# Scaling of the scan's gated groups on ScalarE, other rates of the scan beside the z and memory blocks, and the third head's values two tiles later

## The reference

```python
# first block: the mixer's state-space branch, 32 heads of 64 in 4 groups
z, xbc, dt_f, dt_b, q, k, v, gates = split_cols(h @ w_in, IN_SPLITS)
...
y = y_fwd + y_bwd + d_skip.reshape(SSD_GROUPS, SSD_HPG, 1).astype(xh.dtype) * xh
y = gated_group_rmsnorm(y.reshape(b, s, SSD_INNER), z, ssd_norm_g)
branch_ssd = y @ w_br_ssd
...
def gated_group_rmsnorm(y, z, g):
    v = (y * jax.nn.silu(z)).astype(jnp.float32).reshape(bsz, s, SSD_GROUPS, d // SSD_GROUPS)
    v = v * lax.rsqrt(jnp.mean(v * v, axis=-1, keepdims=True) + EPS)
    return (v.reshape(bsz, s, d) * g.astype(jnp.float32)).astype(y.dtype)
...
# in both blocks, after the mixer: attention over the memory, 4 heads of 256
q = (h @ w_q).reshape(b, s, XATTN_HEADS, XATTN_HEAD_DIM)
scores = jnp.einsum('bqhd,bkhd->bhqk', q, k).astype(jnp.float32) * (XATTN_HEAD_DIM ** -0.5)
probs = jax.nn.softmax(scores, axis=-1).astype(v.dtype)
out = jnp.einsum('bhqk,bkhd->bqhd', probs, v).reshape(b, s, D_MODEL)
return out @ w_o
```

## Time and profile before

| | |
|---|---|
| runs | 2428.92, 2428.44, 2429.64 us |
| profiled execution | 2428.55 us, its span 2426.7 us |
| TensorE (PE) busy | 2396.6 us, 99% |
| its weight loads (PEld) | 1953.8 us, 81% |
| VectorE (DVE) busy | 1262.5 us, 52% |
| ScalarE (ACT) busy | 1001.5 us, 41% |
| GpSimd (POOL) busy | 328.7 us, 14% |
| mean DMA rate | 104 GB/s |
| chain that ended last | PE 93%, DVE 3%, ACT 1% |

### The profile page before, as it was taken

One profiled execution on the slowest core, in us unless ns is written; L12 is line 12 of the kernel. 1 busy time (PEld: TensorE's weight loads), 2 busy tenths in 40 slices (PEclk: granted clock), 3 DMA queues, 4 the chain that ended last, 5 costly groups with the idle time before them and its releaser, 6 DMA issues.

```text
span 2426.7 us, 30328 instructions
## 1 busy us (share of the span) xinstructions
PE 2396.6 (99%) x12040; PEld 1953.8 (81%) x12040; DVE 1262.5 (52%) x1897; ACT 1001.5 (41%) x1628; POOL 328.7 (14%) x254
## 2 busy tenths in 40 slices
PE   8999999999999999999999999999999999999998
PEld 7777778777888888888888888888887888888887
DVE  5688746478764455444333544333677555433422
ACT  7766654235563344333223333222544444322321
POOL 0000000555100101111102111100022201111100
PEclk9999999999999999999999999999999999999999
DMA  6221325323665232332322332222322232333321
GB/s 202 77 70 46 93 96 179 110 78 110 194 204 206 96 105 70 104 98 89 98 98 96 96 105 91 91 96 87 112 62 69 78 113 80 94 96 104 104 96 53
DMA packets 171486, 251.65 MB, mean 104 GB/s; under 512 B 11344, under 2 KB 88400, under 8 KB 171344
## 3 DMA queue, kind: packets, MB, share of 16 engines
q1 hardware_dynamic: 170192, 247.61, 32.1%
q10 hardware_dynamic: 1152, 2.10, 0.2%
HBM read 231.83 MB, written 16.78 MB: 102 GB/s over the span
## 4 chain that ended last, share of the span: by engine, by line
PE 93%; DVE 3%; ACT 1%; issue 1%; DMA 0%; POOL 0%; SPq 0%; POOLq 0%; DVEq 0%; ACTq 0%
PE bank L1132 92%; PE bank L1236 1%; DVE wlo L1946 1%; PE bank L1259 0%; DVE T L1954 0%; ACT xp L1797 0%; PE bank L1360 0%; ACT whi L1478 0%; DMA zb<-scr_z 0%; DVE macc L1946 0%; DVE W L1946 0%; PE bank L1384 0%; PE bank L1195 0%; DVE ml L1954 0%; DMA raw<-in_w_in 0%
## 5 line engine op out<-in xcount | busy, mean ns | idle before, releaser
L1132 PE MATMUL bank<-xh,whi 128*128 128x512 f32 x1784 | 709.8, 398 | 7.9 <-DVE wlo L1946 7.9
L1132 PE MATMUL bank<-xh,wlo 128*128 128x512 f32 x1784 | 696.2, 390 | 0.0
L1132 PE MATMUL bank<-xl,whi 128*128 128x512 f32 x1784 | 695.4, 390 | 0.0
L1946 DVE TENSOR_TENSOR wlo<-raw,whi 128x1024 fp32r<-128x1024 f32 (+2 forms) x406 | 500.7, 1236 | 338.0 <-ACT whi L1478 337.7
L1478 ACT ACTIVATE whi<-raw 128x1024 fp32r<-128x1024 f32 (+2 forms) x406 | 419.4, 1038 | 516.4 <-PE bank L1132 509.5
L1132 PEld LDWEIGHTS bank<-xh,whi 128*128 128x128 f32 x1784 | 335.4, 188 | 94.4 <-issue 20.2
L1132 PEld LDWEIGHTS bank<-xh,wlo 128*128 128x128 f32 x1784 | 335.1, 188 | 71.3
L1132 PEld LDWEIGHTS bank<-xl,whi 128*128 128x128 f32 x1784 | 335.8, 188 | 65.2
L1946 DVE TENSOR_TENSOR T<-bank,R 128x512 f32<-128x512 f32 x86 | 59.0, 688 | 344.3 <-PE bank L1132 344.3
L1132 PE MATMUL bank<-hh,whi 128*128 128x512 f32 x528 | 205.4, 389 | 0.0
L1132 PE MATMUL bank<-hl,whi 128*128 128x512 f32 x528 | 205.4, 389 | 0.0
(11 more groups left out here) (353 smaller groups left out, 3486.4 us busy)
## 6 DMA issues: line engine op xcount, KB each, us to landing
raw<-in_w_in SPq DMA_DIRECT2D x92, 512.0 KB, 3.6
raw<-in_w_ffn_in SPq DMA_DIRECT2D x88, 256.0 KB, 3.2
raw<-in_ffn_gate SPq DMA_DIRECT2D x88, 256.0 KB, 2.8
raw<-in_ffn_up SPq DMA_DIRECT2D x88, 256.0 KB, 3.1
raw<-in_ffn_down SPq DMA_DIRECT2D x44, 512.0 KB, 3.6
raw<-in_w_ffn_out SPq DMA_DIRECT2D x22, 512.0 KB, 3.5
raw<-in_w_xattn_kv SPq DMA_DIRECT2D x16, 512.0 KB, 4.3
raw<-in_w_kv_mem SPq DMA_DIRECT2D x16, 512.0 KB, 4.8
```

The source lines that it names most:

```text
L1132: return e.matmul(out, l, r, start=start, stop=stop, skip_group_check=skip)
L1946: return e.tensor_tensor(out, a, b, op)
```

## The change

The scaling of a group is split in two: `y_inverse` (VectorE's reciprocal) keeps the old place, and `y_scale` becomes four ScalarE copies with a scale, two points later. The scan's rate is 3.5 instead of 3.6 beside `z0` to `z2`, 2.8 beside `z3`, and 2.0 instead of 1.9 beside the memory's blocks. In the attention over the memory `v2`, `t3` and `v3` come two tiles later.

```diff
             for g in means:
                 step("y_mean", g)
-                soon(2, "y_scale", g)
+                soon(2, "y_inverse", g)
+                soon(4, "y_scale", g)
...
-        scan = start(ssd(), 3.6)
+        scan = start(ssd(), 3.5)
         for g in range(4):
             if g == 3:
+                scan[1] = 2.8
                 start(prepare(1, 4), 4)
             gemm(f"z{g}", ev_z(g))
         pace[0] = 0.5
-        scan[1] = 1.9
+        scan[1] = 2.0
...
-                for what in ("t0", "t1", "v0", "", "v1") if hs[0] == 0 else ("t2", "", "v2", "t3", "", "v3"):
+                for what in ("t0", "t1", "v0", "", "v1") if hs[0] == 0 else ("t2", "", "", "", "v2", "t3", "", "v3"):
...
@@ in scalar() @@
+            def y_scale(g):
+                w.wait_ge(*at("y inverse", g))
+                for c in range(4):
+                    ins = copy(xg[g][:, c, :], xg[g][:, c, :], ss[:, 4 * g + c:4 * g + c + 1])
+                ins.then_inc(*up("y_act", ("y scaled", g)))
...
@@ in vector() @@
-            def y_scale(g):
+            def y_inverse(g):
                 s = ss[:, 4 * g:4 * g + 4]
                 w.wait_ge(*at("y sqrt", g))
                 e.reciprocal(s, s).then_inc(*up("y_scaled", ("y inverse", g)))
-                w.wait_ge(*at("y inverse", g))
-                for c in range(4):
-                    ins = ts(xg[g][:, c, :], xg[g][:, c, :], s[:, c:c + 1], None, ALU.mult)
-                ins.then_inc(*up("y_scaled", ("y scaled", g)))
```

More of the change, by code:

```diff
@@ L1927, in scalar @@
                     "o_split": o_split, "dt": dt, "cum": cum, "difference": difference, "cb": cb, "state": state_, "decay": decay, "z_out": z_out,
-                    "z_square": z_square, "y_mean": y_mean, "y_turn": y_turn, "bs_out": bs_out, "m_split": m_split,
+                    "z_square": z_square, "y_mean": y_mean, "y_scale": y_scale, "y_turn": y_turn, "bs_out": bs_out, "m_split": m_split,
                     "mv_out": mv_out, "kv_split": kv_split, "xq_out": xq_out, "x_scores": x_scores, "x_turn": x_turn, "x_pv": x_pv, "ffn_gate": ffn_gate,
@@ L2647, in vector @@
                     "state": state_, "decay": decay, "decayed": decayed, "y_add": y_add, "across": across_, "z_silu": z_silu, "z_gate": z_gate,
-                    "y_mean": y_mean, "y_scale": y_scale, "y_turn": y_turn, "bs_out": bs_out, "bs_lo": bs_lo, "m_lo": m_lo, "m_sum": m_sum,
+                    "y_mean": y_mean, "y_inverse": y_inverse, "y_turn": y_turn, "bs_out": bs_out, "bs_lo": bs_lo, "m_lo": m_lo, "m_sum": m_sum,
                     "mk_out": mk_out, "kv_lo": kv_lo, "xq_out": xq_out, "x_scores": x_scores, "x_turn": x_turn, "x_scale": x_scale, "x_pv": x_pv,
```

## The result

| | before | after |
|---|---|---|
| median of 8 runs each, side by side | 2428.93 us (2428.44 to 2429.64) | 2436.32 us (2435.44 to 2437.72) |
| ratio | | 1.0031, 95% interval 1.0021 to 1.0040 |
| profiled execution | 2428.55, span 2426.7 | 2435.53, span 2433.7 |
| TensorE's idle time, all waits over 0.05 us added up | 22.95 us | 25.17 us |
| granted clock at 1.2 GHz, the end of the program left out | nowhere | three stretches of 3.41 us, from 597.9, 604.7 and 676.4 |

The kernel is 7.4 us slower, outside the predicted range and on the other side. The span grew by 7.0 us, of which TensorE's idle time is 2.2; the other 4.8 are in its busy time.

The account below looks back on a forecast made before the run. TensorE, busy 2396.6 of 2426.7 us, was taken to bound the kernel; 3.3 + 1.6 + 1.1 - 2.1 + 0.1 = 4.0 us gained gave 2424.9 us. Own range 2423 to 2427; 8 in 10, 2419.0 to 2428.4.

Parts of the forecast that it names:

- Attention, +3.3: Attention over the memory: moving v2, t3 and v3 two tiles later removes both TensorE waits for xpl, gaining 3.3 us.
- Scaling, +1.6: Scaling moved to ScalarE: the 1.64 us wait at spread in mkv10 goes with nothing lost, gaining 1.6 us.
- z2, +1.1: Third z block: with points at 3.5 the wlo comes a point earlier, gaining 1.1 of the 1.28 us wait.
- z3 and mkv10, -2.1: Fourth z block and first mkv10 tiles: idle grows by 3.6 us, GpSimd relief returns 1.5, a loss of 2.1.
- The rest of the memory, +0.1: Memory blocks after mkv10: the 0.38 us wait near 658 weighed against gatings meeting memory pieces in mkv13, gaining 0.1 us.
- A: Rival, chance 0.28: in z3 GpSimd's blocking goes and VectorE drops off the path; z3 term +2 to +4.9, 2421 to 2418.
- B: Rival, chance 0.10: VectorE's debt in z3 is paid in full, z3 term -5; time 2427.8, no change.
- C: Rival, chance 0.05: at scan_over leftover points drain with no tile beside them; slower, 2439.4 with four points left.

## Why the prediction was wrong, step by step

From the profiles, the change in idle time by part, in us: attention -3.3, the wait at `spread` -1.6, z2 -0.45, z3 and the first tiles of `mkv10` +1.2, `mkv13` and the start of `mkv20` +5.7, the copies ahead of `Rm` +0.75; with TensorE's busy time, +4.8, that is the span's 7.0 within 0.1. The prediction expected a gain of 4.0.

- **Attention, +3.3: right.** Both waits went, and none came back in `xo`.
- **Scaling, +1.6: right on the wait, wrong in the sum.** The wait at `spread` went, with copies of 0.63 us as estimated (5.01 us for eight). With the new rates it would have gone anyway: the rates alone show no wait there. And "TensorE might stand 0 to 1 us" for the copies ahead of `Rm` was written down and not counted; it is the 0.75 at 692.04, and 3.9 us (2.36 and 1.55) where the ring was gone and the copies stood as they are.
- **z2, +1.1: 0.45.** The wait became 0.83 us at 517 instead of 1.28 at 540, again with a `wlo` (1.94 us, at 512.98) ahead of the "chosen".
- **z3 and mkv10, -2.1: the count right, the price not.** VectorE was busy without a gap from 578.4 to 598.8, as counted, and idle time rose from 4.87 to 6.10 us (7.0 predicted). The help hoped for from GpSimd (1.5 us taken) came about as expected: the seven `macc` of the first memory alone took 4.6 us instead of 5.9. But the idle time came in two pieces of 3.51 and 2.24 (and one of 0.35) instead of four of at most 1.77, and the clock fell twice. Nor is all of it VectorE's backlog, as the prediction has it: ahead of the eviction that ended the 2.24, VectorE itself stood 2.44 us, from 598.9 to 601.3, for ScalarE's root of the norm (1.81 us before). With that the 2.8 cost 4.9 us, the very end of the term's bounds. The clock stood in no term.
- **The rest of the memory, +0.1: the step that failed.** The text says "in `mkv13` gatings and the second memory's pieces now meet, with weights three pairs ahead", and takes bounds of +0.4 and -1. It read the room from means (VectorE 59.42 and ScalarE 51.69 of 85 us) and never laid the points down tile by tile. At 2.0 the scan takes 0.5 a tile, one point for every pair of weights, so the points keep the tile on which they start; the account of 61.2 at `mkv12` puts all of them on the second tile, where `w_lo`, the memory's pieces and `w_hi` are. In the kernel before those of `mkv13` are on the first. Then "chosen" stands behind a `w_lo` whose `w_hi` was written ahead of the last point's exponentials; on the second tile it stands behind the one whose `w_hi` waits for them. Measured: 6.07 us of idle time and 3.4 at the low clock instead of 0.38; and 9.4 us where nothing else was changed. (In `mkv12` the points are on second tiles in both kernels, and neither waits in it; six of the second memory's eight pieces `ml` start only after 658 in the kernel before. Whether the ring needs them was not tried.) "Three pairs ahead" covers the weights' use, not the side banks, of which `seg` has two.
- **Rivals.** A did not come: the idle time of z3 and `mkv10` grew. B's size is what the 2.8 cost in the end, though by way of the clock. C was the only slower one, at 0.05, and was not it: from 700 to 745 us TensorE is busy all the time, so no point was drained uncovered. The right rival, that the order of ScalarE and VectorE closes to a ring, was not among them. The parts don't add either: by medians attention and scaling gain 4.4, the rates cost 9.0, together 4.6, and the change cost 7.4.

What would have shown it blind: the planner's list is deterministic, so writing out the tiles of `mkv13` with both rates, and following one point round both queues (4.63 us, from durations that the trace of before has, against 4.0), was possible before the run.

## What to carry to other kernels

When a rate of interleaved work is changed, lay out on which tile each piece falls before and after, for every stage: a rate that divides the period evenly keeps the pieces on one place, and the place can be worth more than the work. Two in-order engines that feed each other form a ring as soon as one turn of their queues passes through both, so compare the turn's length with the bottleneck's work per period, and don't go by busy shares. Price a wait on TensorE together with the granted clock behind it.

## What was not expected of the hardware

The granted clock. It fell to 1.2 GHz for 3.41 us, or two or three times that, behind or within waits of 3.51, 2.91 and 2.92, and behind waits of 2.36, 2.30, 2.26 and 2.24 us, and in two kernels also behind one of 1.81 and of 1.90, while waits of 1.75 to 1.77 left it full in seven. In the kernel with 0.475 added it fell at 606.4, with the same waits ahead of it as before (0.70, 1.11, 1.29), where the kernel before kept it full. So at this size the length of the last wait alone does not decide it; what does was not settled.

Eight copies with a scale took 5.01 us on ScalarE, 0.63 each, while VectorE took 2.72 and 1.67 us for four of the same shape in the kernel that put them off: the same two durations, one after the other, as at their old place. Why VectorE's first four are slower was not tried.
